# A third plain up pair, a down tile in two passes, and ScalarE copying the last mixer level

## The chip, the cores and the metric

One core of one Trainium2 chip. The metric is the device time of one execution of the whole program in microseconds (us). Engines are named as in the profile: PE is the matmul engine (TensorE), PEld its weight loads, DVE is VectorE, ACT is ScalarE, POOL is GpSimd, and SP only issues loads.

## The reference, cut to what matters

Two trunk layers run on 640 tokens: 512 latent tokens and 128 context tokens, which share the weights. Each layer normalizes x, projects it, runs four mixers in parallel (two attentions, and two gated linear recurrences, of which `chunked_gla` is the core), merges them by gates, adds to x, normalizes again and runs a ConvFFN. All is float32. The parts that the change touches:

```
scores = einsum('bnthk,bnshk,bntshk->bnhts', q, k, decay)   # within a block, masked to t >= s

h2 = rms_norm(x, norm2_g) * (1 + sc2) + sh2
u  = h2 @ w_up                       # 1024 -> 2 x 2816
u  = sum(up[:, j:j + t] * conv_w[j] for j in range(3)) + conv_b
a, g = split(u, 2)
x  = x + g2 * (silu(g) * a) @ w_down # 2816 -> 1024
```

## The kernel before, in words

Activations lie transposed: 128 channels on the partitions, 640 tokens along the row. A float32 product is made of three matmuls on rounded operands: with a value split into a rounded part ("hi") and its remainder ("lo"), hi x hi, lo x hi and hi x lo are added up in PSUM. ACT makes every hi part with a copy that rounds, DVE makes every lo part by subtracting hi from the value, and PE waits for both. Each matmul takes 128x128 weights and 320 tokens.

**Up stage.** The 2816 up channels are 22 pairs of tiles, j = 0 to 21, an `a` tile and a `g` tile each. The first N_PLAIN = 2 pairs are plain products (`two_products`, `up`, lines 789 to 791): 96 matmuls a pair. The other 20 (`strassen`, L1238 to L1240) trade matmuls for sums: a pair is seven parts of 12 matmuls, 84 in all. For this they need, once for a layer, four sums of blocks of the activation, called T here (T1 to T4), and for every pair three sums of weight blocks.

- POOL makes `weight_sums(s)` (L722 to L727, four instructions) when the weight chunk of pair s has landed, for s = 0 ahead of everything else of this stage. It then waits for the whole normalized h, adds hi and lo up again (L740) and makes the T operands (L743 to L748), then `weight_sums(1)`, and so on.
- ACT rounds weights (`up_unit` L1669, `round_sums` L1758 to L1764), rounds T (`round_t` L1768), applies the centre tap of the convolution (`centre` L1777) and the SiLU (L1782).
- DVE makes the lo parts (`up_lo` and `sums_lo`, both through L1991; `t_rest` L2403), the outer taps (`taps` L2374 and L2378), the product `gated` (L2386), and in the Strassen pairs the sums between parts (L2421 to L2459).
- Before that, DVE and ACT make h in eight tiles of 128 channels, one after the other (L1963 to L1979 on DVE, L1354 and L1363 on ACT); PE's pair 0 follows them tile by tile.

Weight chunks go through four slots of RING, loaded by SP as slots come free. A chunk's slot is free when the first matmul of the next chunk has run. Chunk j of the up stage takes the slot of the fourth chunk before it, so up chunk 2 follows the third of the four chunks of the output projection, and up chunk 3 the fourth.

**Down stage.** Eight output tiles, written as two iterations of four. Each takes 22 channel tiles f = 0 to 21 of silu(g) x a. ACT rounds each f (`round_d` L1787), DVE makes its remainder (`rest_d` L2416). For each f in turn, PE runs six matmuls: hi x hi, hi x lo and lo x hi for both token halves. The weights of a tile come in two units of 11 f (`down_unit` L1673 on ACT, `down_lo` on DVE). The first tile waits at each f for `rest_d` of that f; in the later tiles everything is there.

**Mixer, gated recurrences.** For each of three units (x = 0, 1, 2; the third has four heads, the others two) the scores are made in eight passes: pass 0, and one for each of seven levels, whose blocks double in size. PE makes the scores of a head in PSUM (L1116) and goes on with pieces of the merge products (`fill`). DVE's `keep` puts the blocks of the level into SCORE, with a copy under a mask (L2191), and counts `sc_kept`; PE's next scores, and behind the last level the transposes L1128, wait for that count. Between these calls DVE and ACT serve the merge: ACT a gate (L1620) and the rounding of the next weights (L1583), DVE the gating and the lo part.

The order on each engine is written out by hand; there is no scheduler. Everything here happens once in each of the two layers.

Of the kernel before, what the change touches and what calls it, by code (L numbers as in the profile page):

```python
# [12 lines left out]
P = 128  # L13
# [86 lines left out]
N_PLAIN, N_STRASSEN = 2, FT - 2  # L100
# [187 lines left out]
def build(nc, A, O):  # L288
    ctx = ExitStack()
    with ctx:  # L290
# [105 lines left out]
        W_SUMS = [WHI_R[:, 2560:4096], WHI_R[:, 1024:2560]]  # L396
# [30 lines left out]
        D_HI = [V_R[:, T * k:T * (k + 1)] for k in range(7)] + [HH_R[:, k, :] for k in range(KT)] + [HL_R[:, k, :] for k in range(7)]  # L427
# [117 lines left out]
        def tiles_of(w, n=P):  # L545
            return w.rearrange("p (k n) -> p k n", n=n)
# [213 lines left out]
        def _(pe):  # L760
# [3 lines left out]
            for l in range(DEPTH):  # L764
# [462 lines left out]
                def up(j):  # L1227
                    for h in range(2):
                        g = G_UP + 2 * j + h
                        wait_room(pe, l, g)  # L1230
                        lo_ready(U_UP + 2 * j + h)
                        w_hi, w_lo = up_weights(j, h, W2[h])
                        product(use(g)[0], w_hi, w_lo, h_hi, h_lo, KT, h == 0)
# [50 lines left out]
                up(1)  # L1284
                for s in range(N_STRASSEN):
                    strassen(s)
                with pe.Fori(0, 2) as it:
                    for j in range(4):
                        g = G_DOWN + j
                        wait_room(pe, l, g, it)  # L1290
                        for h in range(2):
                            lo_ready(U_DOWN + 2 * j + h, it * 8)

                            def d_lo_ready(k):
                                pe.wait_ge(d_ready, l * FT + (11 * h + k + 1))

                            product(use(g)[0], tiles_of(W_DN[h]), raw(RING_R, DOWN + 2 * j + h, 0, P, P, 11), lambda k: D_HI[11 * h + k],
                                    lambda k: ZT_R[:, 11 * h + k, :], 11, True, d_lo_ready if j == 0 else None, h == 0, h == 1)

        @block.scalar  # L1300
        def _(act):
# [17 lines left out]
            for l in range(DEPTH):  # L1319
# [305 lines left out]
                for x, g in enumerate(GLA):  # L1625
                    before = sum(y[6] for y in GLA[:x])
                    gates_before(AT[x, "turn"])
# [167 lines left out]
                silu(0)  # L1795
                round_sums(0, 0)
# [3 lines left out]
                wait_event(act, l, EV_UP + 2)  # L1800
                round_sums(0, 2)
                centre(1, 0)
                round_t("t4", 4)
                wait_event(act, l, EV_UP + 3)
                round_t("t1", 1)
                centre(1, 1)
                for s in range(N_STRASSEN):
                    if s:
                        centre(s + 1, 0)
                    wait_part(act, l, s, 0)  # L1810
                    act.activation(FIRST_A[s % 2], PS[:, use(G_UP + 2 * (N_PLAIN + s))[0], EDGE - H2:EDGE], ACT.Copy).then_inc(first_kept, 1)
                    silu(s + 1)
                    if s + 1 < N_STRASSEN:
                        round_sums(s + 1, 0)
                        round_sums(s + 1, 1)
                        wait_part(act, l, s, 5)
                        round_sums(s + 1, 2)
                    else:
                        down_unit(0)
                        wait_part(act, l, s, 5)  # L1820
                        for a, b in ((0, 4), (4, 8)):
                            act.dma_start(XT[:, a:b, :], XD.rearrange("p (k t) -> p k t", k=KT)[:, a:b, :]).then_inc(x_again, 16)
                        round_d(0, 2)
                    centre(s + 2, 1)
                round_d(2, 4)
# [3 lines left out]
                round_d(4, 6)  # L1829
                silu(FT - 1)  # L1830
                round_d(6, FT)
# [29 lines left out]
        def _(v):  # L1861
# [12 lines left out]
            for l in range(DEPTH):  # L1874
# [307 lines left out]
                def keep(x, groups, h, p):  # L2182
                    nonlocal cnt
                    v.wait_ge(sc_full, l * NSC + (cnt + 1))
                    ps = pair(3 - cnt % 2)[:, 0:T].rearrange("p (n t) -> p n t", n=NT)
                    if p == 0:
                        ins = nv.tensor_copy(SCORE[:, h], ps)
                    else:
                        v.sem_inc(scores_seen, 1)
                        m = MASK[:, p, :].rearrange("p (o t) -> p o t", o=1).to_broadcast([P, NT, P])  # L2190
                        ins = nv.copy_predicated(SCORE[:, h], m, ps)  # L2191
                    ins.then_inc(sc_kept, 1)
                    cnt += 1
                    merge_before(AT[x, 2 * groups * p + h])
# [231 lines left out]
                gated(0)  # L2426
                sums_lo(0, 0)
# [3 lines left out]
                taps(1, 0)  # L2431
# [3 lines left out]
                for s in range(N_STRASSEN):  # L2435
# [3 lines left out]
                    taps(s + 1, 1)  # L2439
# [3 lines left out]
                    if s:  # L2443
                        taps(s + 1, 0)
                    else:
                        gated(1)
# [9 lines left out]
                    else:  # L2456
                        down_lo(0)
                    wait_part(v, l, s, 5)
# [3 lines left out]
                    else:  # L2462
                        rest_d(0, 2)
                last_sum(N_STRASSEN - 1)
                rest_d(2, 4)
                taps(FT - 1, 1)
                down_lo(1)
                rest_d(4, 6)
                taps(FT - 1, 0)
                rest_d(6, FT)  # L2470
# [124 lines left out]
```

## Time and profile before

| | us |
|---|---|
| median of 3 executions | 2533.16 |
| lowest and highest | 2529.04, 2534.22 |
| the profiled execution, its own time | 2532.05 |
| its span, first to last instruction | 2529.9 |

The mean granted TensorE clock over the span is 0.974 of full speed (2.4 GHz). All positions in time below are microseconds from the start of the profiled span, and are those of the second layer, where its up stage begins near 2060 and its down stage near 2357; the first layer shows the same pattern.

### The profile page before, as it was taken

The page shows a single profiled execution, that of the slowest core. Times are in us where ns is not written, and L with a number is a line of the kernel's source. Part 1 is how long each engine was busy: PE and PEld are TensorE (multiplying, and loading weights), DVE is VectorE, ACT ScalarE, POOL GpSimd, SP SyncE. Part 2 cuts the span into 40 slices and gives each one's busy share as a digit, 9 for nine tenths or more (in the row PEclk, how much of TensorE's full clock was granted, in tenths as well). Part 3 has the DMA queues.
Part 4 walks back from the last instruction along what each step waited for, and adds up shares of the span by engine and source line. Part 5 has one row for each costly group of instructions (what it writes and reads, how often), then busy time and mean ns, then how long its engine had stood idle before and what let it go on. Part 6 is the DMA issues. An engine that isn't in the chain of part 4 may idle for free. (4 is left out here: it accounts for less than half of the span.)

```text
span 2529.9 us, 49558 instructions
## 1 busy us (share of the span) xinstructions
PE 2391.7 (95%) x21546; PEld 2224.6 (88%) x21546; DVE 1524.1 (60%) x2310; ACT 1009.8 (40%) x1384; POOL 333.3 (13%) x223
## 2 busy tenths in 40 slices
PE   5999998899999799999989999979999998999998
PEld 4999776888999799999989997768899988999998
DVE  4134476886745788883241536768775658888621
ACT  4244554322242555561143536542222544555410
POOL 0000000000000455530000000000000016555000
PEclk8999998999999999999999999989999999999999
DMA  8545111212245233333244431111222632332321
GB/s 277 190 151 184 37 46 32 54 44 53 64 144 183 59 84 84 88 100 99 75 141 126 133 93 42 48 30 51 54 65 81 212 100 62 92 89 74 99 80 65
DMA packets 326509, 239.32 MB, mean 95 GB/s; under 512 B 18272, under 2 KB 317344, under 8 KB 325024
## 3 DMA queue, kind: packets, MB, share of 16 engines
q1 hardware_dynamic: 317584, 211.32, 28.5%
q10 hardware_dynamic: 8720, 24.99, 2.9%
q8 instruction: 162, 2.65, 0.4%
q14 instruction: 43, 0.35, 0.0%
HBM read 220.68 MB, written 15.60 MB: 93 GB/s over the span
## 5 line engine op out<-in xcount | busy, mean ns | idle before, releaser
L789 PE MATMUL PS<-HH_split,WHI_split 128*128 128x320 f32 x1888 | 600.3, 318 | 13.2 <-DVE HL_split L1966 10.4
L791 PE MATMUL PS<-HH_split,RING_split 128*128 128x320 f32 x1856 | 578.0, 311 | 0.0
L790 PE MATMUL PS<-HL_split,WHI_split 128*128 128x320 f32 x1632 | 508.7, 312 | 0.0
L1991 DVE TENSOR_TENSOR RING_split<-RING,WHI_split 128x1024 fp32r<-128x1024 f32 (+2 forms) x162 | 224.9, 1390 | 262.6 <-ACT WHI_split L1673 185.1
L789 PEld LDWEIGHTS PS<-HH_split,WHI_split 128*128 128x128 f32 x1888 | 359.3, 190 | 26.6 <-issue 15.2
L790 PE MATMUL PS<-ZT_split,WHI_split 128*128 128x320 f32 x1208 | 375.9, 311 | 0.0
L791 PEld LDWEIGHTS PS<-HH_split,RING_split 128*128 128x128 f32 x1856 | 352.9, 190 | 0.0
L790 PEld LDWEIGHTS PS<-HL_split,WHI_split 128*128 128x128 f32 x1632 | 310.9, 191 | 0.3
L722 POOL TENSOR_TENSOR ST<-RING 128x512 f32<-128x512 f32 x20 | 31.9, 1595 | 1824.0 <-DMA RING<-in_w_up 1725.1
L790 PEld LDWEIGHTS PS<-ZT_split,WHI_split 128*128 128x128 f32 x1208 | 229.5, 190 | 0.0
L1239 PE MATMUL PS<-BIG_split,WHI_split 128*128 128x320 f32 x640 | 200.3, 313 | 0.0
L1998 DVE TENSOR_TENSOR RING_split<-RING,WHI_split 128x1024 fp32r<-128x1024 f32 x52 | 62.2, 1223 | 228.6 <-ACT WHI_split L1382 228.2
L789 PE MATMUL PS<-V_split,WHI_split 128*128 128x320 f32 x536 | 169.8, 317 | 8.9 <-DVE ZT_split L2416 8.9
L791 PE MATMUL PS<-V_split,RING_split 128*128 128x320 f32 x544 | 171.0, 314 | 0.0
L1238 PE MATMUL PS<-V_split,WHI_split 128*128 128x320 f32 x480 | 150.5, 313 | 18.6 <-DVE BIG_split L2403 13.8
L1620 ACT ACTIVATE WHI<-PS 128x640 f32<-128x640 f32 x48 | 33.8, 705 | 263.2 <-PE PS L791 263.0
L1673 ACT ACTIVATE WHI_split<-RING 128x1408 fp32r<-128x1408 f32 x32 | 44.1, 1379 | 214.4 <-PE PS L791 214.4
L1543 ACT ACTIVATE BIG<-PS,NMX 128x768 f32<-128x768 f32 (+1 forms) x120 | 94.1, 791 | 76.4 <-DVE NMX L2092 76.3
L1239 PEld LDWEIGHTS PS<-BIG_split,WHI_split 128*128 128x128 f32 x640 | 122.2, 191 | 0.0
L2191 DVE COPY_PREDICATED BIG<-MASK,PS 128x640 f32<-128x640 uint8 x112 | 98.3, 884 | 35.4 <-PE PS L1116 34.6
L2092 DVE TENSOR_REDUCE NMX<-PS 128x1 f32<-128x768 f32 (+1 forms) x120 | 93.3, 819 | 37.5 <-PE PS L1004 33.9
L789 PEld LDWEIGHTS PS<-V_split,WHI_split 128*128 128x128 f32 x536 | 101.9, 190 | 11.9 <-DVE ZT_split L2416 8.9
(305 smaller groups left out, 5481.5 us busy)
## 6 DMA issues: line engine op xcount, KB each, us to landing
RING<-in_w_in SPq DMA_DIRECT2D x96, 512.0 KB, 4.0
RING<-in_w_up SPq DMA_DIRECT2D x88, 512.0 KB, 5.0
RING<-in_w_ada SPq DMA_DIRECT2D x80, 512.0 KB, 6.3
RING<-in_w_down SPq DMA_DIRECT2D x32, 384.0 KB, 3.6
RING<-in_w_in SPq DMA_DIRECT2D x40, 256.0 KB, 3.3
RING<-in_w_down SPq DMA_DIRECT2D x32, 320.0 KB, 4.0
RING<-in_w_out SPq DMA_DIRECT2D x16, 512.0 KB, 4.6
ZT<-in_w_ada SPq DMA_DIRECT2D x8, 1024.0 KB, 9.2
```

The costliest lines, as they stand in the source:

```text
L789: release(pe.matmul(out, w_hi, hi[:, a:b], start=begin, stop=False), fresh and a == 0)
L790: pe.matmul(out, w_hi, lo[:, a:b], start=False, stop=False)
L791: ins = pe.matmul(out, w_lo, hi[:, a:b], start=False, stop=end)
L1238: release(pe.matmul(out, w_hi[k], hi[:, k, :], start=not onto and k == 0, stop=False, skip_group_check=onto), fresh and k == 0)
L1239: pe.matmul(out, w_hi[k], lo[:, k, :], start=False, stop=False, skip_group_check=onto)
L1543: act.activation(PROB[g % 3][m][:, 0:n], pair(m)[:, 0:n], ACT.Exp, bias=NMX[:, g % 3, m:m + 1], accum_out=SUMS[:, g % 3, m:m + 1]).then_in ...
L1620: act.activation(GATE[m % 2], acc(use(g)[0]), ACT.Sigmoid).then_inc(gemm_free[use(g)[0]], 1)
L1673: act.activation(W_DN[q % 2], RING[:, (DOWN + q) % N_SLOT, 0:11 * P], ACT.Copy).then_inc(hi_made, 1)
L1991: nv.tensor_tensor(rest, value, as_f32(hi), ALU.subtract).then_inc(lo_made, 1)
L1998: nv.tensor_tensor(z_raw(RING_R, l, c, j), z_raw(RING, l, c, j), as_f32(w_z(u, 256 if kind in ("t4", "t1") else P)), ALU.subtract).then_in ...
L2092: nv.tensor_reduce(NMX[:, g % 3, m:m + 1], pair(m)[:, 0:keys(g // NS) * P], AX.X, ALU.max, negate=True).then_inc(nmax_ready, 1)
L2191: ins = nv.copy_predicated(SCORE[:, h], m, ps)
```

## The change

Three edits, made together.

1. **N_PLAIN is 3.** Pair j = 2 becomes a plain pair, so a layer has 19 Strassen pairs. ACT, DVE and PE get its units behind those of pair 1 (`up_unit(2, .)`, `up_lo(2, .)`, `taps(1, .)` and `gated(1)`), all ahead of the rounding of the sums and of T. `weight_sums(0)` now reads up chunk 3, not 2. The `g` weights of pair 2 go to another buffer, and the two buffers of summed weights change places, so that nothing collides.
2. **The first down tile of each iteration runs in two passes** (`down_first`): for f = 0 to 21 four matmuls with the rounded f (hi x hi and lo x hi), then for f = 0 to 21 two matmuls with the remainder. In the last Strassen pair ACT now rounds f = 0 to 10 as the operands of the finished parts come free, and 11 to 13 right behind; D_HI's places are reordered for that. DVE does both halves of the last pair's taps ahead of `down_lo(1)` and of the remainders from f = 4 on.
3. **ACT copies the blocks of the last mixer level** (the seventh, two blocks of 64x64 on each of five token blocks) straight from PSUM into SCORE, without a mask; DVE only goes on with the merge there.

```diff
-N_PLAIN, N_STRASSEN = 2, FT - 2
+N_PLAIN, N_STRASSEN = 3, FT - 3
...
-        D_HI = [V_R[:, T * k:T * (k + 1)] for k in range(7)] + [HH_R[:, k, :] for k in range(KT)] + [HL_R[:, k, :] for k in range(7)]
+        D_HI = [V_R[:, T * k:T * (k + 1)] for k in range(4)] + [HH_R[:, k, :] for k in range(KH)] + [HL_R[:, k, :] for k in range(KH)] + \
+               [V_R[:, T * k:T * (k + 1)] for k in range(4, 7)] + [HH_R[:, k, :] for k in range(KH, KT)] + [HL_R[:, k, :] for k in range(KH, 7)]
...
+                def down_first(it):
+
+                    p = use(G_DOWN)[0]
+                    wait_room(pe, l, G_DOWN, it)
+                    for f in range(FT):
+                        h, k = f // 11, f % 11
+                        w_hi, w_lo = down_weights(h)
+                        if k == 0:
+                            lo_ready(U_DOWN + h, it * 8)
+                        pe.wait_ge(d_hi, l * FT + (f + 1))
+                        for a, b, o in HALVES:
+                            out = PS[:, p, o:o + HALF]
+                            release(pe.matmul(out, w_hi[:, k, :], D_HI[f][:, a:b], start=f == 0, stop=False), k + a == 0)
+                            pe.matmul(out, w_lo[:, k, :], D_HI[f][:, a:b], start=False, stop=False)
+                    for f in range(FT):
+                        h, k = f // 11, f % 11
+                        pe.wait_ge(d_ready, l * FT + (f + 1))
+                        for a, b, o in HALVES:
+                            ins = pe.matmul(PS[:, p, o:o + HALF], down_weights(h)[0][:, k, :], ZT_R[:, f, a:b], start=False, stop=f == FT - 1)
+                        if k == 10:
+                            ins.then_inc(pe_done, 1)
...
+                    for h in range(2 * g[6]):
+                        seen = 2 * NPASS * before + 2 * g[6] * LEVELS + h
+                        gates_before(AT[x, 2 * g[6] * LEVELS + h])
+                        act.wait_ge(sc_full, l * NSC + seen + 1)
+                        act.wait_ge(sc_kept, l * NSC + seen)
+                        ps = pair(3 - seen % 2)[:, 0:T].rearrange("p (n t) -> p n t", n=NT)
+                        for ks, qs in level_blocks(LEVELS):
+                            ins = act.activation(SCORE[ks, h, :, qs], ps[ks, :, qs], ACT.Copy)
...
+                    if p == LEVELS:
+                        cnt += 1
+                        merge_before(AT[x, 2 * groups * p + h])
+                        return
```

**Where instructions move.** DVE at the beginning of the up stage, from the product of pair 0 on (rows with WORK are the taps, RING_split, CACHE and ST_split are lo parts of weights, BIG_split are remainders of T). Before:

```order
L2386 TENSOR_TENSOR ZT<-WORK 128x640
L1991 TENSOR_TENSOR RING_split<-RING,CACHE_split 128x1024
L1991 TENSOR_TENSOR ST_split<-ST,WHI_split 128x1536
L2403 TENSOR_TENSOR BIG_split<-BIG,V_split 128x4x320 x2
L2374 SCALAR_TENSOR_TENSOR WORK<-PS,COLS,WORK 128x511
```

Now, from the lo part of pair 2's `g` weights on; behind pair 0's product come also, ahead of these rows, pair 2's `a` weights and four tap instructions:

```order
L2039 TENSOR_TENSOR RING_split<-RING,WHI_split 128x1024
L2426 SCALAR_TENSOR_TENSOR WORK<-PS,COLS,WORK 128x511
L2426 SCALAR_TENSOR_TENSOR WORK<-PS,COLS,WORK 128x127
L2430 SCALAR_TENSOR_TENSOR WORK<-PS,COLS,WORK 128x511
L2430 SCALAR_TENSOR_TENSOR WORK<-PS,COLS,WORK 128x127
L2438 TENSOR_TENSOR ZT<-WORK 128x640
L2039 TENSOR_TENSOR RING_split<-RING,CACHE_split 128x1024
L2039 TENSOR_TENSOR ST_split<-ST,WHI_split 128x1536
L2455 TENSOR_TENSOR BIG_split<-BIG,V_split 128x4x320 x2
```

So two lo parts, two halves of a pair's taps (eight instructions) and one product now stand ahead of the first lo part of a Strassen pair.

ACT in the last Strassen pair (WORK rows with PS are `centre`, 128x1408 is a unit of down weights, reads of ZT are `round_d`). Before:

```order
L1673 ACTIVATE WHI_split<-RING 128x1408
L1822 DMA BIG<-x_kept 128x2560 x2
L1787 ACTIVATE V_split<-ZT 128x640 x2
L1777 ACTIVATE WORK<-PS,COLS 128x640
L1787 ACTIVATE V_split<-ZT 128x640 x2
```

Now:

```order
L1708 ACTIVATE WHI_split<-RING 128x1408
L1822 ACTIVATE V_split<-ZT 128x640 x4
L1822 ACTIVATE HH_split<-ZT 128x640 x4
L1822 ACTIVATE HL_split<-ZT 128x640 x3
L1872 DMA BIG<-x_kept 128x2560 x2
L1812 ACTIVATE WORK<-PS,COLS 128x640
```

Eleven roundings now stand between the first unit of down weights and the loads of x, where before there was none.

ACT in the second unit of the recurrences, behind its last gate and weights (WHI rows). Before:

```order
L1620 ACTIVATE WHI<-PS 128x640
L1583 ACTIVATE WHI_split<-RING 128x1280
L1630 ACTIVATE BIG<-PS 128x640 x2
L1620 ACTIVATE WHI<-PS 128x640
L1583 ACTIVATE WHI_split<-RING 128x1280
```

Now:

```order
L1644 ACTIVATE WHI<-PS 128x640
L1607 ACTIVATE WHI_split<-RING 128x1280
L1658 ACTIVATE BIG<-PS 64x5x64 x4
L1665 ACTIVATE BIG<-PS 128x640 x2
L1644 ACTIVATE WHI<-PS 128x640
```

The four copies of 64 partitions serve two heads; they follow the same gate and weights as the two copies L1665 that were next before.

## Rows read from the trace of the kernel before

**Rows 1.** the page, part 1: busy us (share of the span) and instructions of each engine.

```profile
PE 2391.7 (95%) x21546; PEld 2224.6 (88%) x21546; DVE 1524.1 (60%) x2310; ACT 1009.8 (40%) x1384; POOL 333.3 (13%) x223
```

**Rows 2.** waits of PE: engine, line, waited for: us in total, times, longest.

```profile
PE PS L1238 <- DVE BIG_split L2403: 13.9, 3, 6.9
PE PS L789 <- DVE ZT_split L2416: 8.9, 6, 2.9
```

**Rows 3.** timeline of PE, second layer: start, us, line, [idle before].

```profile
2106.54 0.60 PE L1238 MATMUL PS<-V_split,WHI_split 128*128 128x320 f32 x1 [6.88 <-DVE BIG_split L2403]
...
2112.49 0.41 PE L1238 MATMUL PS<-V_split,WHI_split 128*128 128x320 f32 x1 [2.41 <-DVE RING_split L1991]
```

**Rows 4.** stretches: length, busy (instructions) of PE, PEld, DVE, ACT, POOL; granted clock; DMA.

```profile
2106.50:2109.90 3.40, 3.36 (x12) 3.17 (x12) 3.36 (x4) 0.87 (x2) 3.32 (x2) 0.50 0.00 0
2128.50:2337.90 209.40, 209.40 (x1430) 209.40 (x1429) 175.64 (x272) 105.81 (x119) 119.95 (x86) 1.00 0.30 83
2362.30:2373.10 10.80, 7.07 (x28) 6.26 (x28) 10.77 (x15) 10.80 (x18) 2.01 (x1) 0.68 0.37 120
```

**Rows 5.** timeline of SP's queue, second layer: loads of up chunks 2 and 3.

```profile
2042.75 1.10 SPq L586 DMA_DIRECT2D RING<-in_w_up  x2
...
2067.38 1.00 SPq L586 DMA_DIRECT2D RING<-in_w_up  x2
```

**Rows 6.** timeline of POOL, second layer: weight sums, then the T operands.

```profile
2048.95 1.30 POOL L722 TENSOR_TENSOR ST<-RING 128x512 f32<-128x512 f32 x1 [914.14 <-DMA RING<-in_w_up]
2050.21 1.30 POOL L723 TENSOR_TENSOR RING<-RING 128x512 f32<-128x512 f32 x1
...
2081.83 7.16 POOL L740 TENSOR_TENSOR BIG<-HH_split,HL_split 128x640 f32<-128x640 f32 x4 [27.11 <-DVE HL_split L1963]
...
2099.53 4.28 POOL L748 TENSOR_TENSOR BIG<-BIG 128x1280 f32<-128x1280 f32 x1
```

**Rows 7.** timeline of DVE beside those weight sums.

```profile
2046.90 0.82 DVE L1920 TENSOR_TENSOR WORK<-WORK 128x640 f32<-128x640 f32 x1
...
2050.65 1.54 DVE L1920 TENSOR_TENSOR WORK<-WORK 128x640 f32<-128x640 f32 x1
```

**Rows 8.** timeline of DVE, second layer, up stage.

```profile
2083.95 1.01 DVE L2374 SCALAR_TENSOR_TENSOR WORK<-PS,COLS,WORK 128x511 f32<-128x511 f32 x2 [2.20 <-ACT WORK L1777]
...
2090.32 2.40 DVE L2386 TENSOR_TENSOR ZT<-WORK 128x640 f32<-128x640 f32 x1 [0.81 <-ACT WORK L1782]
...
2103.92 4.96 DVE L2403 TENSOR_TENSOR BIG_split<-BIG,V_split 128x1280 fp32r<-128x1280 f32 x2 [2.85 <-POOL BIG L748]
...
2113.76 1.48 DVE L2403 TENSOR_TENSOR BIG_split<-BIG,HH_split 128x1280 fp32r<-128x1280 f32 x1
...
2118.01 0.82 DVE L2386 TENSOR_TENSOR ZT<-WORK 128x640 f32<-128x640 f32 x1 [0.41 <-ACT WORK L1782]
...
2119.74 1.22 DVE L1991 TENSOR_TENSOR RING_split<-RING,HL_split 128x1024 fp32r<-128x1024 f32 x1
```

**Rows 9.** timeline of DVE: the last sum of the third Strassen pair.

```profile
2148.54 0.49 DVE L2421 TENSOR_TENSOR PS<-PS,CACHE 128x320 f32<-128x320 f32 x1
```

**Rows 10.** timeline of DVE, second layer, start of the down stage.

```profile
2375.79 5.23 DVE L2416 TENSOR_TENSOR ZT_split<-ZT,HL_split 128x640 fp32r<-128x640 f32 x7
2380.94 1.62 DVE L1991 TENSOR_TENSOR RING_split<-RING,WHI_split 128x1408 fp32r<-128x1408 f32 x1
```

**Rows 11.** timeline of ACT, the same stretch.

```profile
2369.46 4.49 ACT L1787 ACTIVATE HL_split<-ZT 128x640 fp32r<-128x640 f32 x7
...
2385.30 1.38 ACT L1673 ACTIVATE WHI_split<-RING 128x1408 fp32r<-128x1408 f32 x1 [8.30 <-PE PS L791]
```

**Rows 12.** timeline of PE, second layer, second GLA unit, behind its last level.

```profile
1810.01 0.55 PE L1128 MATMUL PS<-CONST,WORK 128*128 128x128 f32 x3 [1.57 <-DVE BIG L2191]
```

**Rows 13.** timeline of ACT there, and ACT's copy of 320 columns.

```profile
1802.26 1.27 ACT L1583 ACTIVATE WHI_split<-RING 128x1280 fp32r<-128x1280 f32 x1 [1.05 <-PE PS L791]
...
2125.39 0.43 ACT L1811 ACTIVATE V<-PS 128x320 f32<-128x320 f32 x1
```

More of the change, by code:

```diff
@@ L1292, in _ @@
                             lo_ready(U_DOWN + 2 * j + h, it * 8)
[L1294 to L1298, printed above, removed]
+                            product(use(g)[0], *down_weights(2 * j + h), lambda k: D_HI[11 * h + k],
+                                    lambda k: ZT_R[:, 11 * h + k, :], 11, True, None, h == 0, h == 1)
         @block.scalar
@@ L1626, in _ @@
                     before = sum(y[6] for y in GLA[:x])
+                    for h in range(2 * g[6]):
[6 more added lines that the diff above has]
+                            ins = act.activation(SCORE[ks, h, :, qs], ps[ks, :, qs], ACT.Copy)
+                            if ks.start == 0:
+                                step.mark(ins)
+                        ins.then_inc(sc_kept, 1)
                     gates_before(AT[x, "turn"])
@@ L1795, in _ @@
                 silu(0)
+                wait_event(act, l, EV_UP + 2)
+                up_unit(2, 0)
+                centre(1, 0)
+                wait_event(act, l, EV_UP + 3)
+                up_unit(2, 1, w=W_APART)
+                centre(1, 1)
+                silu(1)
                 round_sums(0, 0)
@@ L2426, in _ @@
                 gated(0)
+                up_lo(2, 0)
+                taps(1, 0)
+                up_lo(2, 1, w=W_APART)
+                taps(1, 1)
+                gated(1)
                 sums_lo(0, 0)
@@ L2430, in _ @@
                 t_rest(1, "t3")
-                taps(1, 0)
+                taps(2, 0)
                 sums_lo(0, 2)
@@ L2438, in _ @@
                         last_sum(s - 1)
-                    taps(s + 1, 1)
+                    taps(N_PLAIN + s - 1, 1)
                     v.wait_ge(first_kept, l * N_STRASSEN + s + 1)
@@ L2457, in _ @@
                         down_lo(0)
+                        rest_d(0, 3)
                     wait_part(v, l, s, 5)
@@ L2462, in _ @@
                     else:
-                        rest_d(0, 2)
+                        rest_d(3, 4)
                 last_sum(N_STRASSEN - 1)
-                rest_d(2, 4)
                 taps(FT - 1, 1)
+                taps(FT - 1, 0)
                 down_lo(1)
-                rest_d(4, 6)
-                taps(FT - 1, 0)
-                rest_d(6, FT)
+                rest_d(4, FT)
                 v.wait_ge(x_again, l * 32 + 32)
```

44 lines of the change are left out of this document (27 added, 17 removed).

## The prediction, made before the change was run

> **What bounds the kernel now.** I read the page's busy shares first. PE is busy for 95% of the span, DVE for 60%, ACT for 40% [rows 1], so over the whole PE sets the time, and a change counts by the PE idle time that it removes, less the matmuls that it adds. The waits of PE say where it idles: 13.9 us in total before Strassen matmuls for remainders of T, 8.9 us before down matmuls for remainders of f [rows 2]. The timeline shows the first in the second layer: idle for 6.88 us, one part of 12 matmuls, idle for 2.41 us [rows 3]. The stretches add what idling does afterwards: those 12 matmuls took 3.40 us at a granted clock of 0.50, which is the 1.2 GHz level, where the steady Strassen pairs run 1430 matmuls in 209.4 us at 1.00, the 2.4 GHz level [rows 4], 0.1466 us each. So 12 matmuls are 1.76 us at the full clock and cost some 1.6 us more at the lower one. In between, PE had waited for an operand; the stretch in the down stage with such waits has a clock of 0.68 [rows 4].
>
> Both places are bounded by DVE, which makes remainders without a break, and by POOL, which makes T before it. I therefore lay out DVE's list in the new order. All places are of the second layer, and I count each gain twice.
>
> **Edit 1, the third plain pair.** A pair costs 96 x 0.1466 = 14.07 us instead of 84 x 0.1466 = 12.32: 1.76 us more matmul work for each layer. What it buys is 14 us of PE work while T is made. How much of that comes out depends on when the last remainder of T is ready.
>
> (a) A move that the diff hides. POOL's first weight sums started at 2048.95, when up chunk 2 had landed [rows 6], 6.2 us after SP issued its load at 2042.75 [rows 5]. They now need chunk 3, whose load is issued at 2067.38 [rows 5], since its slot is held by the output projection until up pair 0 begins. So they start at about 2067.4 + 6.2 = 2073.6, and lie in the middle of the normalization, where POOL was idle for 27 us [rows 6].
>
> (b) POOL and DVE hold each other up. While POOL's weight sums ran, a DVE addition of two SBUF operands took 1.54 us instead of 0.82 [rows 7]: it began at 2050.65, and ended 0.7 us after POOL's 2050.21 + 1.30 = 2051.51 [rows 6], so it was let in when POOL's instruction was over. Likewise in the up stage, a product took 2.40 us beside POOL and 0.82 without it [rows 8]. The taps, with one operand in PSUM, took 1.01 us for each two beside POOL [rows 8] and are not held up. In the normalization, DVE's instructions read two SBUF operands; half are additions or products as in rows 7, half have a scalar operand as well, a form that the trace never shows beside a busy POOL. I take them to be held up as well, as the nearest rows are. POOL's four sums of 1.30 us [rows 6] then go in one by one between DVE's, 5.2 us, of which about 1.1 falls into time in which DVE waits for ACT anyway. The last h tile is done 4.1 us later, near 2085.9 instead of 2081.8. If only the additions are held up, it is 1.3 us later.
>
> On this form the Trainium skill speaks too. "SBUF — State Buffer", section "Who interferes with whom", says that a DVE instruction with two SBUF inputs contends with a GpSimd instruction that reads SBUF, and that the second to issue blocks for the whole of the other; by that all of the normalization's instructions are held up and edit 1 gains 2.4 us, where with the additions alone held up it would gain 5.3; the trace agrees for the additions (1.54 us against 0.82), and shows nothing for the rest.
>
> (c) T. POOL takes from 2081.83 to 2099.53 + 4.28 = 2103.81 for it [rows 6], 22 us with DVE's interruptions. It now ends near 2107.9.
>
> (d) DVE's list. From the last h tile at 2081.8 to the end of the last remainder of T it needed 2113.76 + 1.48 - 2081.8 = 33.5 us [rows 8]. The new list holds in the same place two more lo parts (1.22 each), two halves of taps (four times 1.01) and a product (0.82) [rows 8], together 7.2 us. The 2.85 us for which DVE waited for T4 [rows 8] are filled by that work. Three of the new instructions have two SBUF operands and wait for POOL; followed instruction by instruction, with POOL and DVE in turn, this adds 1.2 us. So 33.5 + 7.2 - 2.85 + 1.2 = 39.1, and the last remainder is ready at 2085.9 + 39.1 = 2125.0.
>
> (e) PE then has four of the seven parts left: 48 x 0.1466 = 7.0 us, 0.35 us until the end is seen, and 1.3 us for a lower clock after its waits of about 3 and 1 us before parts 2 and 3 (less than one whole part's 1.6). The first Strassen pair, j = 3, ends at 2133.7 and the next, j = 4, at 2146.1. Before, j = 4 was the third Strassen pair and its last sum began at 2148.54 [rows 9]. **Gain: 2.4 us for each layer.** The ends: 5.3 if (b) gives 1.3 us instead of 4.1; a loss of 1.5 if PE, idle for some 6 us inside pair 0 while h is late, runs that pair at the lower clock too, so that everything behind starts about 2 us later, and POOL's turns cost DVE 2 us more.
>
> **Edit 2, the down tile.** DVE worked without a break from the last Strassen pair until its lo part for the second tile ended at 2380.94 + 1.62 = 2382.6 [rows 10]; PE ended its first tile at about 2385.0, 0.3 us before ACT saw it at 2385.30 [rows 11]. Now PE can use what is rounded. Pass 1 has 88 matmuls, 12.9 us from 2357.5, with one wait of about 0.9 us for the second half's weights; it ends near 2371.3. ACT's roundings, 0.64 us each [rows 11], keep ahead of it, eleven being done before. Pass 2 then follows `rest_d`, 5.23/7 = 0.75 us each [rows 10], and needs only 0.29 us for each f: it ends right behind DVE. DVE's list gets 4 x 0.75 = 3.0 us shorter, since four remainders now lie in the last Strassen pair, and has about 1.5 us of waiting for ACT's last two `centre`, which stand behind 14 roundings. So the second tile's lo part ends at 2382.6 - 3.0 + 1.5 = 2381.1, and the second tile starts at 2381.2 instead of 2385.0: 3.8 us. Pass 2 works PE at under half, and the clock may be down when the second tile starts: I take off 0.8 us. The first unit's weights are given free only 22 matmuls (3.2 us) before the tile's end, and ACT's 1.38 [rows 11] and DVE's 1.62 [rows 10] with handovers take 3.4; in the first iteration DVE's list hides this, in the second it is 0.1 to 0.2 us, within rounding. **Gain: 3.0 us**, ends 1.0 (a low clock for most of the second tile's first half) and 4.2.
>
> **Edit 3, the last level.** PE waited for 1.57 us before the transposes of the second unit, for DVE's masked copy of the second head, which stood behind a merge step [rows 12]. In the other two units PE did not wait there. ACT is through with its merge step at 1802.26 + 1.27 = 1803.5 [rows 13]. Four copies of 320 columns at 0.43 [rows 13] end by 1805.3, and PE's fill covers until 1808.3, so the wait goes. In the third unit the second head's copy stands behind a gate and weights, and ends some 0.4 us before PE asks for it. **Gain: 1.5 us**, ends 1.0 and 1.6. DVE's freed time in the other units is worth nothing: PE does not wait for it there.
>
> **Sum.** 2.4 + 3.0 + 1.5 = 6.9 for a layer, 13.8 us for two. The profiled execution's own time of 2532.05 (2529.9 of it the span) becomes 2518.3. The median of the runs stands 1.1 us above it; against it I forecast **2519.3 us**. About 0.2% (5 us) is what a measurement of this kernel can tell from no change.
>
> **Rivals.**
> - *Only additions are held up in the normalization.* For it: no row shows the other form beside POOL. Against it: all rows with two SBUF operands show the exclusion. Then 5.3 + 3.0 + 1.5 = 9.8, twice: 2513.6.
> - *DVE eats the third pair.* The list before the last remainder grows by 7.2 us; if POOL's turns cost 2.4 us more than I found, PE idles as long as the new pair lasts and edit 1 gives nothing: 2 x 4.5 = 9.0, 2524.2. For it: DVE is already the last to finish there.
> - *The down tile does not get shorter, as the change says it does.* Pass 2 hangs on the same 22 remainders; if the clock is low in the second tile's first half, 0.5 us are left: 2 x 4.4 = 8.8, 2524.4.
> - *Slower: the weight sums inside the normalization.* One mechanism, POOL's and DVE's turns from (b), with its place between 2073 and 2125. Edit 1 becomes a loss when the last remainder of T ends later than 2127.4, and the whole change when later than 2131.9, 6.9 us behind my figure. That needs DVE to be held up by a POOL instruction of 2.9 us at three more places. At 2134 it costs 2.1 us a layer net: 2537.4. Against it: DVE's own work is known, and each turn lets DVE in after one POOL instruction.
>
> **Chances.** Forecast 0.43, additions only 0.20, third pair eaten 0.17, down tile not shorter 0.13, slower 0.07. All but the last are faster; in the third and fourth together, or with edit 3 short of its gain, the result comes within 0.2%. So faster 0.83, same 0.10, slower 0.07. The range reaches from both good ends (2533.2 - 2 x 11.1 = 2511) to the third and fourth rival together (about 2529): 2510 to 2529.
>
> **What would show it.** In the changed profile: POOL's first sums near 2073 and DVE's normalization instructions of up to 1.9 us beside them; the last h tile near 2086; PE's 6.9 us wait before the second Strassen part gone and waits of about 3 and 1 us before the third and fourth in its place; the second down tile starting some 24 us after the last Strassen part instead of 27.7; no wait before the second unit's transposes. A last h tile later than 2090, or waits before Strassen parts of over 6 us in sum, would make edit 1 and the forecast wrong.

## The result and the profile after

The changed kernel takes 2512.65 us (median of 4 runs, 2511.16 to 2513.83) against 2532.15 us of the kernel before (4 runs, 2529.04 to 2534.22): a ratio of 0.9927, 95% interval 0.9915 to 0.9939. It is 18.5 us faster by the ratio, and the forecast of 2519.3 us promised 13.8 us. The sign and the range held, and the size did not: a quarter of the gain by the ratio, and a third of it by the stages below, was not foreseen.

Where it lies is read by stage, from the starts of the same matmul in the two traces. The stretch "up" goes from the first product with h2 to the last Strassen matmul; "down" goes from there to the 300th matmul after it; what is left is the mixers, where only edit 3 works, and there the row goes from the transposes of the first gated-recurrence unit to those of the third (200.9 and 199.6 us before, 197.5 and 196.3 after).

| us for each layer | forecast | layer 1 | layer 2 |
|---|---|---|---|
| edit 1, up: 290.3 before, 286.4 after | 2.4 | 3.8 | 3.9 |
| edit 2, down: 52.4 before, 49.35 after | 3.0 | 3.1 | 3.1 |
| edit 3, last mixer level | 1.5 | 3.35 | 3.35 |

The sum over both layers is 20.6 us; the spans differ by 2529.9 - 2509.4 = 20.5.

The busy times on the page of the changed kernel (answers to [rows 1]): PE is still at 95%, with 5 us less of busy time than before and the rest of the gain out of its idle time.

```profile
PE 2386.7 (95%) x21570; PEld 2220.7 (88%) x21570; DVE 1505.5 (60%) x2284; ACT 1019.9 (41%) x1412; POOL 318.3 (13%) x213
```

The waits of PE in the changed kernel (as [rows 2]: in total, times, longest):

```profile
PE PS L790 <- DVE HL_split L2014: 17.8, 6, 4.9
...
PE PS L1239 <- DVE RING_split L2039: 2.5, 2, 1.3
...
PE PS L1239 <- DVE BIG_split L2455: 1.6, 2, 0.8
PE PS L1310 <- DVE ZT_split L2468: 1.4, 8, 0.2
...
PE PS L1304 <- DVE RING_split L2039: 0.9, 2, 0.4
...
PE PS L1239 <- DVE ST L2506: 0.4, 2, 0.2
```

The 13.9 us before Strassen matmuls for remainders of T are 1.6, and the 8.9 us for remainders of f are 1.4. In exchange PE now waits longer for the h tiles, 17.8 us in the first line; the same line of the kernel before, in the same view:

```profile
PE PS L789 <- DVE HL_split L1966: 10.4, 6, 4.9
```

The longest of 4.9 us in that line stands in another stage, near 1296; in pair 0 of the second layer, PE's longest wait for an h tile behind the first was this one:

```profile
2075.89 0.42 PE L789 MATMUL PS<-HH_split,WHI_split 128*128 128x320 f32 x1 [1.21 <-DVE HL_split L1966]
```

**Edit 1 in the trace.** In the second layer everything starts 13.72 us earlier by now: the first product with h2 began at 2053.11 in place of 2066.83. That number is added where a time is compared with the forecast. POOL's timeline (start, us, engine, line, operation, tiles), second layer:

```profile
2059.27 1.63 POOL L723 TENSOR_TENSOR ST<-RING 128x512 f32<-128x512 f32 x1 [936.13 <-DMA RING<-in_w_up]
2060.86 1.32 POOL L724 TENSOR_TENSOR RING<-RING 128x512 f32<-128x512 f32 x1
2062.25 1.73 POOL L726 TENSOR_TENSOR ST<-ST,RING 128x512 f32<-128x512 f32 x1
2064.06 1.60 POOL L728 TENSOR_TENSOR ST<-ST,RING 128x512 f32<-128x512 f32 x1
...
2089.11 2.97 POOL L749 TENSOR_TENSOR BIG<-BIG 128x1280 f32<-128x1280 f32 x1
```

DVE beside it, and later the last remainder of T and the last sum of pair j = 4:

```profile
2059.00 2.05 DVE L2027 SCALAR_TENSOR_TENSOR WORK<-BIG,A,WORK 128x512 f32<-128x512 f32 x2
2060.97 1.89 DVE L2024 TENSOR_TENSOR WORK<-BIG,WORK 128x640 f32<-128x640 f32 x1
2062.78 3.02 DVE L2014 SCALAR_TENSOR_TENSOR HL_split<-WORK,MOD,HH_split 128x512 fp32r<-128x512 f32 x2
2065.72 1.00 DVE L2027 SCALAR_TENSOR_TENSOR WORK<-BIG,A,WORK 128x512 f32<-128x512 f32 x2
...
2070.55 0.82 DVE L2011 TENSOR_TENSOR HL_split<-BIG,HH_split 128x640 fp32r<-128x640 f32 x1 [1.43 <-ACT BIG L1387]
...
2108.75 1.49 DVE L2455 TENSOR_TENSOR BIG_split<-BIG,HH_split 128x1280 fp32r<-128x1280 f32 x1
...
2130.90 0.49 DVE L2473 TENSOR_TENSOR PS<-PS,CACHE 128x320 f32<-128x320 f32 x1
```

The sums start at 2059.27 (2073.0 on the clock of before). The form that no row of before showed beside POOL, with a scalar operand and two SBUF operands, took 2.05 and 3.02 us for two pieces while POOL's sums ran, and 1.00 once they were over. PE's timeline shows what that does to the products, and what is left in front of the Strassen parts:

```profile
2065.85 0.63 PE L790 MATMUL PS<-HH_split,WHI_split 128*128 128x320 f32 x1 [4.90 <-DVE HL_split L2014]
...
2107.49 0.41 PE L1239 MATMUL PS<-V_split,WHI_split 128*128 128x320 f32 x1 [1.20 <-DVE RING_split L2039]
...
2110.29 0.41 PE L1239 MATMUL PS<-HH_split,WHI_split 128*128 128x320 f32 x1 [0.79 <-DVE BIG_split L2455]
...
2114.28 0.41 PE L1239 MATMUL PS<-V_split,WHI_split 128*128 128x320 f32 x1 [0.21 <-DVE ST L2506]
...
2361.31 0.56 PE L1310 MATMUL PS<-ZT_split,WHI_split 128*128 128x320 f32 x2 [0.18 <-DVE ZT_split L2468]
2362.85 0.63 PE L790 MATMUL PS<-V_split,WHI_split 128*128 128x320 f32 x1 [0.97 <-DVE RING_split L2039]
```

The last two rows are the end of edit 2's first down tile and the start of the second one. PE follows DVE's last remainders there, and then waits for the lo part of the second tile's weights, which DVE makes right behind them:

```profile
2361.19 1.61 DVE L2039 TENSOR_TENSOR RING_split<-RING,WHI_split 128x1408 fp32r<-128x1408 f32 x1
```

The stretches (busy time and count of each engine, then the granted clock): behind the late h tile, the first Strassen pair, the start of the second down tile, and the third mixer unit's projection.

```profile
2066.20:2069.10 2.90, 2.90 (x12) 2.90 (x12) 2.90 (x6) 1.89 (x4) 0.00 (x0) 0.50 0.02 6
2102.60:2118.10 15.50, 13.30 (x88) 12.51 (x87) 14.92 (x21) 7.20 (x8) 0.00 (x0) 1.00 0.25 69
2362.80:2366.10 3.30, 3.25 (x12) 3.25 (x13) 2.55 (x3) 0.49 (x1) 0.00 (x0) 0.51 0.32 97
1817.90:1821.40 3.50, 3.50 (x41) 3.46 (x30) 3.31 (x5) 1.20 (x2) 0.00 (x0) 1.00 0.00 0
```

The last of these, in the kernel before, at the same place in the program:

```profile
1830.10:1833.70 3.60, 3.60 (x30) 3.56 (x19) 3.42 (x5) 0.52 (x2) 0.00 (x0) 0.53 0.02 5
```

So the clock was lower (0.50, the 1.2 GHz level) behind the h tile's new wait, and not in the first Strassen pair, where the forecast had put it; and the third mixer unit's projection, 20 us after the wait that edit 3 removes, runs at the 2.4 GHz level now, where it ran at the 1.2 GHz level before.

### The profile page after: what moved, and what is told of

It reads as the page before. It is cut to its first block and busy times, and to the rows that moved or that the text cites. A ratio compares the mean times of both kernels' runs of the same rounds, so it can differ in the third digit from the quotient of the medians.

```text
span 2509.4 us, 49596 instructions
## 1 busy us (share of the span) xinstructions
PE 2386.7 (95%) x21570; PEld 2220.7 (88%) x21570; DVE 1505.5 (60%) x2284; ACT 1019.9 (41%) x1412; POOL 318.3 (13%) x213
## 5 line engine op out<-in xcount | busy, mean ns | idle before, releaser
L790 PE MATMUL PS<-HH_split,WHI_split 128*128 128x320 f32 x1888 | 598.6, 317 | 20.0 <-DVE HL_split L2014 17.8
L791 PE MATMUL PS<-HL_split,WHI_split 128*128 128x320 f32 x1696 | 528.4, 312 | 0.0
L2039 DVE TENSOR_TENSOR RING_split<-RING,WHI_split 128x1024 fp32r<-128x1024 f32 (+2 forms) x164 | 235.9, 1440 | 265.0 <-ACT WHI_split L1708 183.5
L791 PEld LDWEIGHTS PS<-HL_split,WHI_split 128*128 128x128 f32 x1696 | 322.8, 190 | 0.3
L791 PE MATMUL PS<-ZT_split,WHI_split 128*128 128x320 f32 x1032 | 320.5, 311 | 0.0
L791 PEld LDWEIGHTS PS<-ZT_split,WHI_split 128*128 128x128 f32 x1032 | 195.3, 189 | 0.0
L1240 PE MATMUL PS<-BIG_split,WHI_split 128*128 128x320 f32 x608 | 187.8, 309 | 0.0
L790 PE MATMUL PS<-V_split,WHI_split 128*128 128x320 f32 x480 | 151.9, 316 | 2.0 <-DVE RING_split L2039 2.0
L792 PE MATMUL PS<-V_split,RING_split 128*128 128x320 f32 x488 | 153.4, 314 | 0.0
L1239 PE MATMUL PS<-V_split,WHI_split 128*128 128x320 f32 x456 | 141.3, 310 | 2.9 <-DVE RING_split L2039 2.5
L2243 DVE COPY_PREDICATED BIG<-MASK,PS 128x640 f32<-128x640 uint8 x96 | 84.8, 883 | 34.7 <-PE PS L1117 34.5
L1239 PE MATMUL PS<-HH_split,WHI_split 128*128 128x320 f32 x304 | 94.1, 310 | 1.6 <-DVE BIG_split L2455 1.6
```

Of the source, the lines that this page charges most:

```text
L790: release(pe.matmul(out, w_hi, hi[:, a:b], start=begin, stop=False), fresh and a == 0)
L791: pe.matmul(out, w_hi, lo[:, a:b], start=False, stop=False)
L792: ins = pe.matmul(out, w_lo, hi[:, a:b], start=False, stop=end)
L1239: release(pe.matmul(out, w_hi[k], hi[:, k, :], start=not onto and k == 0, stop=False, skip_group_check=onto), fresh and k == 0)
L1240: pe.matmul(out, w_hi[k], lo[:, k, :], start=False, stop=False, skip_group_check=onto)
L2039: nv.tensor_tensor(rest, value, as_f32(hi), ALU.subtract).then_inc(lo_made, 1)
```

## The experiments

Two executions of the same code differ: up to the first product with h2 the kernel before and `pair_only` are the same program, and their profiled executions stood 2.2 us apart there (831.27 and 833.51). The stretches "up" and "down" on the other hand repeat within 0.1 us from layer to layer in most kernels, so small effects are read from them. All numbers in the table are for one layer, layer 1 and layer 2; the ratio is to executions of the kernel before that were taken beside each kernel (their medians are 2529.4 to 2532.2 us), and "low clock" counts the matmuls of the second down tile's first 68 that stood 0.2 to 0.3 us apart.

| kernel | median us | ratio (95%) | up | down | low clock |
|---|---|---|---|---|---|
| before | 2532.15 | | 290.3, 290.3 | 52.4, 52.4 | 0, 0 |
| after | 2512.65 | 0.9927 (0.9915 to 0.9939) | 286.5, 286.4 | 49.3, 49.4 | 10, 11 |
| after_again | 2510.08 | 0.9922 (0.9907 to 0.9937) | 286.4, 286.5 | 49.4, 49.3 | 10, 10 |
| pair_only | 2523.86 | 0.9971 (0.9961 to 0.9980) | 286.5, 286.5 | 52.6, 52.8 | 0, 0 |
| no_down | 2517.69 | 0.9951 (0.9937 to 0.9966) | 286.4, 286.4 | 52.7, 52.8 | 0, 0 |
| one_pass | 2515.76 | 0.9938 (0.9924 to 0.9951) | 286.4, 286.4 | 51.4, 51.4 | 0, 0 |
| no_copy | 2518.95 | 0.9948 (0.9934 to 0.9963) | 286.5, 286.4 | 49.4, 49.5 | 11, 11 |
| copy_only | 2524.93 | 0.9970 (0.9958 to 0.9982) | 290.3, 290.3 | 52.4, 52.4 | 0, 0 |
| copy_x1 | 2522.74 | 0.9969 (0.9957 to 0.9981) | 290.4, 290.2 | 52.5, 52.4 | 0, 0 |
| sums_late | 2512.30 | 0.9928 (0.9914 to 0.9941) | 288.1, 288.1 | 48.0, 47.9 | 1, 1 |
| sums_late_t | 2510.56 | 0.9919 (0.9905 to 0.9932) | 285.6, 285.6 | 49.5, 49.5 | 14, 14 |
| sums1_late | 2509.85 | 0.9917 (0.9903 to 0.9931) | 285.8, 285.8 | 49.5, 49.5 | 14, 14 |
| sums_both_late | 2501.27 | 0.9880 (0.9865 to 0.9895) | 284.3, 284.3 | 48.0, 47.9 | 1, 1 |
| gate_late | 2506.78 | 0.9900 (0.9883 to 0.9918) | 283.5, 283.6 | 49.2, 50.6 | 9, 21 |

**pair_only: edit 1 alone, on the kernel before**, with the lists of ACT, DVE and PE as the change has them.

```diff
-N_PLAIN, N_STRASSEN = 2, FT - 2
+N_PLAIN, N_STRASSEN = 3, FT - 3
...
```

> The kernel before with the first edit alone (three plain pairs). Theory from the two profiles: the last sum of pair j = 4 came 3.9 us earlier for each layer in the changed kernel, so this edit is worth 7.8 us and the time should be near 2524.4 against 2532.2 of before. The prediction's own figure of 2.4 us for each layer would give 2527.4; no gain at all (third pair eaten) 2532. The last h tile should again come about 3.3 us later than before, by POOL's weight sums in the normalization.

The ratio gives 7.3 us (5.1 to 9.9), and "up" is as long as in the changed kernel, 286.5. So the 3.8 to 3.9 us for each layer belong to this edit alone.

**no_down: edit 2 undone**, with one pass and the rounding late.

> The changed kernel with the second edit undone: one pass over the first down tile, rounding late. Theory: the edit is worth what the profiles show from the end of the last Strassen part on, 3.1 us for each layer, so 2512.7 + 6.2 = 2518.9. Rival: the early end of the down tile only moves a wait further back, and the time stays within 2 us of 2512.7.

"Down" is 52.7 and 52.8 against 49.35: 3.4 us for each layer; in time 5 to 8 us, between this kernel and the two measurements of the changed one. The rival falls: what the first tile gains isn't waited for later.

**one_pass: which half of edit 2 carries it.** The rounding stays early, but the tile is made in one pass again.

```diff
-                    down_first(it)
-                    for j in range(1, 4):
+                    for j in range(4):
...
+                            product(use(g)[0], tiles_of(W_DN[h]), raw(RING_R, DOWN + 2 * j + h, 0, P, P, 11), lambda k: D_HI[11 * h + k],
...
```

> The changed kernel with the early rounding kept, but the first down tile in one pass of six matmuls for each f as before. Theory A: VectorE's list sets the end of the tile, so the four early remainders and the early rounding carry the gain; TensorE waits some 4 us for remainder 4, runs some matmuls at the lower clock, and then follows VectorE at 0.88 us for each f against 0.75, so that the second tile starts some 2 us later than with two passes but at the full clock: 1 to 4 us slower than the changed kernel in all. Theory B: the two passes carry it, and without them the edit's 3.1 us for each layer are lost: 6 us slower than the changed kernel.

"Down" is 51.4: 2.0 us more than with two passes, and 1.0 us less than before. PE's timeline of one_pass has one wait, for the first remainder behind those made early:

```profile
2348.02 0.64 PE L790 MATMUL PS<-HH_split,WHI_split 128*128 128x320 f32 x1 [5.46 <-DVE ZT_split L2446]
```

Theory A's range (1 to 4 us) holds at its upper end, and its weights are wrong: what is made early (roundings and four remainders) carries one third of the edit, the two passes two thirds, since they fill that wait with products of the rounded f.

**no_copy, copy_only and copy_x1: edit 3 undone, alone, and alone in the second of the three units.** The edit of copy_x1 in ACT's list (DVE's copy has the same condition; in copy_only it is without it):

```diff
+                    for h in range(2 * g[6] if x == 1 else 0):
...
+                        for ks, qs in level_blocks(LEVELS):
+                            ins = act.activation(SCORE[ks, h, :, qs], ps[ks, :, qs], ACT.Copy)
...
```

> The changed kernel with the third edit undone: VectorE copies the last mixer level again. Theory A: the edit is worth the wait of 1.6 us before the second unit's transposes and, behind it, 13 matmuls of the third unit's output projection at the lower clock (1.5 us), together 3.35 us for each layer: 2512.7 + 6.7 = 2519.4. Theory B, as the prediction had it: the wait alone, 1.5 us for each layer, and the clock has another cause: 2515.7.

> The kernel before with the third edit alone, in all three units. From the two profiles: 3.35 us for each layer, 6.7 us faster than before. By the prediction's term, 1.5 us for each layer, 3.0 us faster. The 1.57 us wait before the second unit's transposes should be gone in both cases; by the first figure the third unit's first output-projection matmuls run 0.147 us apart, by the second 13 of them stay at 0.267 us.

> The kernel before with ScalarE copying the last level in the second unit alone. Theory A: the lower clock in the third unit follows from the wait in the second, so the whole 3.35 us for each layer is there, 6.7 us faster than before, and the third unit's 13 matmuls run at full clock. Theory B: it is the third unit's own copy by VectorE that costs there; then 13 matmuls stay at 0.267 us and the gain is 1.8 us for each layer, 3.6 us.

The ratios give 7.6 us for copy_only (4.6 to 10.6) and 7.8 for copy_x1 (4.8 to 10.9); no_copy lies 5 to 9 us above the changed kernel. Theory A holds in each. Its mark is the granted clock in the third unit's projection, in the second layer of copy_x1:

```profile
1821.90:1825.40 3.50, 3.50 (x39) 3.46 (x26) 3.34 (x5) 1.16 (x2) 0.00 (x0) 1.00 0.01 2
```

And of no_copy:

```profile
1819.90:1823.40 3.50, 3.50 (x22) 3.50 (x15) 3.40 (x5) 0.48 (x2) 0.00 (x0) 0.54 0.01 2
```

In the three kernels with the wait (before, pair_only, no_copy) 12 to 14 matmuls there stood some 0.267 us apart, in both layers; in the eleven without it one or two at most stood 0.25 us apart. Each matmul at 0.267 in place of 0.147 us costs 0.12 us more, so 12 cost 1.45 us. The same 360 matmuls around the place, from 60 before the second unit's transposes on, took 34.8 us in both layers of the three kernels, and 31.5 us in both layers of the eleven. So wait and lower clock come and go together, by an edit in the second unit alone; whether the wait lowers the clock by itself, or by shifting PE's work behind it, no run separates. The copies in the first and third unit give nothing that the times show.

**sums_late: POOL's first weight sums behind T**, on the changed kernel.

```diff
-                weight_sums(0)
                 pool.wait_ge(h_ready, l * 16 + 16)
...
                 pool.tensor_tensor(T_RAW["t4"], T_RAW["t4"], b22, ALU.subtract).then_inc(t_made, 1)
+                weight_sums(0)
```

> The changed kernel with POOL's first weight sums moved behind the four tiles of T. Theory: beside the normalization the sums hold VectorE up, the last h tile comes 3.3 us late and TensorE then runs 12 matmuls at the lower clock, 4.6 us in all for each layer; moved away, h and T come 3.3 us earlier, the sums are made some 2 us before they are needed, and the gain is 3.3 to 4.6 us for each layer: 2503.5 to 2506. Rival: the remainders of the sums become the late ones before the second Strassen part, and what h gains is waited for there: 2512.7, or later.

The theory falls. The last h tile did come 3.3 us earlier (2068.40 - 2053.48 = 14.9 us behind the first h2 product, 2071.37 - 2053.11 = 18.3 in the changed kernel), and the wait on h tiles was 10.4 us in total again. But DVE and ACT stood before the first sums with T finished behind them in their lists, and PE waited there. On DVE's timeline of sums_late:

```profile
2096.02 2.31 DVE L2039 TENSOR_TENSOR RING_split<-RING,CACHE_split 128x1024 fp32r<-128x1024 f32 x1 [5.20 <-POOL ST L728]
```

And on PE's:

```profile
2103.72 0.60 PE L1239 MATMUL PS<-V_split,WHI_split 128*128 128x320 f32 x1 [3.25 <-DVE BIG_split L2455]
```

"Up" is 1.7 us longer; the time stays only because the second down tile ran at the full clock from its start, which shortened "down" by 1.4 us.

**sums_late_t: T2 and T3 before the first sums, in ACT's and DVE's lists.**

```diff
-                round_sums(0, 0)
-                round_sums(0, 1)
                 round_t("t2", 3)
                 round_t("t3", 2)
+                round_sums(0, 0)
+                round_sums(0, 1)
...
```

> As sums_late, with ScalarE and VectorE also taking T2 and T3 before the first weight sums instead of after them. In sums_late VectorE stood for 5.2 us before the first sums' remainder although T was done when that wait began. Theory: filled with T2's and T3's remainders, that wait gives the last remainder of T some 3.5 us earlier than in the changed kernel and a gain of about 3 us for each layer, 6 us against the changed kernel (near 2506.5). Rival: beside POOL's sums each remainder takes as long as POOL's instruction and its own together, the sums get later, and the time stays within 2 us of 2512.5.

"Up" falls by 2.5 us against sums_late, and by 0.8 against the changed kernel: the rival. POOL and DVE took turns. POOL's timeline of sums_late_t:

```profile
2097.89 2.27 POOL L724 TENSOR_TENSOR RING<-RING 128x512 f32<-128x512 f32 x1
2100.24 2.68 POOL L726 TENSOR_TENSOR ZT<-ZT,RING 128x512 f32<-128x512 f32 x1
```

And DVE's beside it:

```profile
2096.74 2.28 DVE L2039 TENSOR_TENSOR RING_split<-RING,CACHE_split 128x1024 fp32r<-128x1024 f32 x1 [2.56 <-POOL ST L728]
2098.94 2.83 DVE L2039 TENSOR_TENSOR ST_split<-ST,WHI_split 128x1536 fp32r<-128x1536 f32 x1
```

POOL's sum of 1.30 us became 2.27 and 2.68, DVE's remainders of 1.22 and 1.75 us became 2.28 and 2.83. These are the *second* weight sums, which nobody needs yet.

**sums1_late and sums_both_late: the second weight sums held back** until three remainders of T are done, in the changed kernel and in sums_late_t. after_again is the changed kernel beside them.

```diff
                     if s + 1 < N_STRASSEN:
+                        if s == 0:
+                            pool.wait_ge(t_lo, l * 4 + 3)
                         weight_sums(s + 1)
```

> The changed kernel once more, on the same chip as the two below, so that they are compared with it directly: a ratio to before of 0.9927 within 0.0012.

> The changed kernel with POOL's second weight sums held back until the third remainder of T is done. In the changed kernel they ran from 2092.0 to 2098.8, and two VectorE instructions beside them took 1.70 instead of 0.82 us and 2.31 instead of 1.22. Theory: VectorE gains those 2.0 us before the last remainder of T, TensorE's waits of 2.2 us before the Strassen parts go, and the time falls by 1.5 to 2 us for each layer, 3 to 4 us. Rival: the second sums, now made some 8 us later, hold up the second Strassen pair, and the time stays or rises.

> As sums_late_t, with the second weight sums held back in the same way. In sums_late_t the h tile was early by 4.5 us for each layer, and 3.4 of that were lost again in front of the Strassen parts, where VectorE's instructions beside the second weight sums took 2.28 instead of 1.22, 2.83 instead of 1.75 and 1.72 instead of 1.22 us. Theory: without these 2.7 us the gain on the changed kernel is 1.1 + 2.5 = 3.6 us for each layer, 7 us. Rival: TensorE waits for the first sums' remainder, which stands behind T's whatever the second sums do, and no more than 1 us for each layer is added to the 2 us in all that sums_late_t gained.

In the first, "up" is 0.65 us shorter instead of 1.5 to 2: the rival, in part. The hold-up has moved to the product of the third pair, which now runs beside the late sums, and PE waits for the sum behind it for 1.1 us instead of 0.2. PE's waits of sums_both_late show the same (in total, times, longest; 0.4, 2, 0.2 in the changed kernel):

```profile
PE PS L1241 <- DVE ST L2508: 2.2, 2, 1.1
```

With both moves "up" is 2.1 us shorter than in the changed kernel, against 3.6 expected: beside that wait, PE waits for 2.2 us in each layer for lo parts of the first Strassen pair's weights (1.2 in the changed kernel), which is the rival in part. The remainders beside which no POOL sum runs are back at their own length (DVE's timeline of sums_both_late):

```profile
2095.76 1.23 DVE L2041 TENSOR_TENSOR RING_split<-RING,CACHE_split 128x1024 fp32r<-128x1024 f32 x1 [2.56 <-POOL ST L728]
2097.27 1.76 DVE L2041 TENSOR_TENSOR ST_split<-ST,WHI_split 128x1536 fp32r<-128x1536 f32 x1 [0.29 <-ACT WHI_split L1799]
...
2107.75 1.70 DVE L2440 TENSOR_TENSOR ZT<-WORK 128x640 f32<-128x640 f32 x1 [0.41 <-ACT WORK L1819]
```

Another 1.4 us for each layer came from the clock of the second down tile, which no theory had. The time of 2501.27 us beats both kernels: 30 us under the one before, 8.8 under after_again. Of these 8.8, the two stretches show 7.0 in both layers together; the rest was not located.

**gate_late: that product behind two of the first Strassen pair's sums**, on sums_both_late.

```diff
                     if s:
                         taps(N_PLAIN + s - 1, 0)
-                    else:
-                        gated(N_PLAIN - 1)
...
                     nv.tensor_tensor(g1, U3, a1, ALU.subtract).then_inc(out_sum, 1)
+                    if s == 0:
+                        gated(N_PLAIN - 1)
```

> As sums_both_late, with VectorE's product of the third plain pair moved from before the sums of the first Strassen pair to behind two of them. In sums_both_late this product ran beside POOL's second weight sums, took 1.70 instead of 0.82 us, and TensorE waited 1.1 us in each layer for the sum behind it. Theory: the 2.2 us of that wait go and the time falls by some 2 us, a ratio to before near 0.987. Rival: the product only holds up the next pair's weight remainders instead, and the ratio stays at 0.988.

"Up" is 0.75 us shorter, and the wait is gone; but the second down tile had 9 and 21 matmuls at the lower clock, and its five runs went from 2500.27 to 2512.55. Whether it is faster stays open.

## Why the prediction was right, and what it mis-sized

- **What bounds the kernel: right.** DVE's and POOL's lists before the first Strassen pair and the first down tile set PE's idle time, and removing it there moved the whole kernel by as much.
- **Edit 1, (a): right.** Sums at 2073.0, forecast 2073.6.
- **(b): right in kind, 0.8 us off.** The form with a scalar operand is held up too, 2.05 and 3.02 us against 1.00, so the rival "only additions" is refuted, although its 2513.6 us is the nearest figure to the result. That is luck: of the 3.4 us for each layer that the forecast missed, 1.85 lie in edit 3 and at most 0.8 in (b). The last h tile ended at 2071.37 + 13.72 = 2085.1; forecast 2085.9. The rule of the Trainium skill, "SBUF — State Buffer", section "Who interferes with whom", by which all of the normalization's instructions are held up, agrees with these rows.
- **(c) and (d): 2.1 and 1.0 us too late.** T ended at 2105.8 (forecast 2107.9) and the last remainder at 2110.24 + 13.72 = 2124.0 (forecast 2125.0).
- **(e): the term that was mis-sized.** It took off 1.3 us for a lower clock after waits of 3 and 1 us. The waits were 1.20 and 0.79 us, and the clock of the stretch was 1.00. The 1.3 and the 1.0 of (d), less some 0.8 us that was not in the sum (PE's wait of 0.21 us is a part of it, the rest was not traced), are the difference between 2.4 and 3.9: the last sum of j = 4 began at 2130.90 + 13.72 = 2144.6, forecast 2146.1, before 2148.54 [rows 9].
- **Edit 2: right in kind, its size in part by luck.** The second tile began 23.3 us behind the last Strassen matmul instead of 27.9, 0.8 us better than forecast, and 11 of its matmuls at the lower clock took 1.3 us back where 0.8 had been taken off; the two misses nearly cancel in 3.1 against 3.0. As forecast, DVE's lo part for the second tile ends (2361.19 + 1.61 = 2362.80) right before that tile begins (2362.85). How the gain divides between early remainders and two passes, the prediction did not say; one_pass does.
- **Edit 3: the step that failed.** "So the wait goes" held; its price did not. "Gain: 1.5 us, ends 1.0 and 1.6" counted the wait of 1.57 us [rows 12] and nothing behind it. With the wait, PE also ran at the lower clock 20 us later: 12 to 14 matmuls at 0.267 us, some 1.45 us more; copy_x1 shows that both go by the edit in the second unit alone. From start to start the wait cost 1.73 us (1808.13 to 1810.01, where now it is 1797.74 to 1797.89), and the term measured 3.35 us. The prediction had looked for clock losses directly behind waits, in the up and down stages alone.
- **The working.** Two slips in it change nothing: the third of POOL's four sums took 1.76 us before, not 1.30, and the new work in (d) adds up to 7.3 us, not 7.2.
- **The rivals.** The third pair was not eaten (edit 1 gave more than forecast, not nothing), the down tile did get shorter, and the weight sums did not make it slower. Their cost is there all the same: the late h tile costs PE a wait of 4.9 us in place of 1.2, and 12 matmuls at the lower clock. sums_late shows why that didn't decide: the time was slack that PE otherwise spends in front of the Strassen parts.

## What to carry to other kernels

When work is taken off a late list, ask what its neighbours on the shared resource do at that time: DVE's instructions on two SBUF operands and POOL's go one at a time here (1.22 us became 2.28 beside POOL), and the best version moved both of POOL's first two weight sums out of DVE's way, the second of them a lookahead that nobody needed yet. That gave 2.1 us for each layer; another 1.4 came with the clock of the second down tile, whose cause is not known. A move that makes one operand early gains nothing until each list on the way stops waiting in its old order. And when a PE wait is priced, read the granted clock of the next PE-heavy stretch too, not only right behind the wait: a wait of 1.6 us was worth 3.35.

## What was not expected of the hardware

The lower clock 20 us behind a short wait is one: in all fourteen kernels, with the wait 12 to 14 slow matmuls, without it one or two at most, while the 1.70 us pause of PE just before them is the same in all. The other is the second down tile. Its start lies 23.3 us behind the last Strassen matmul in every kernel with two passes, with the same waits, yet between none and 21 of its matmuls ran at the lower clock (up to 2.5 us), and the number was nearly the same in both layers of all of them but gate_late. In sums_late the stretch of 3.3 us behind the tile's start holds 22 matmuls at a granted clock of 1.00, where the changed kernel has 12 at 0.51:

```profile
2364.90:2368.20 3.30, 3.27 (x22) 3.27 (x23) 2.55 (x3) 0.47 (x1) 0.00 (x0) 1.00 0.44 128
```

So the one matmul that the table counts for sums_late and sums_both_late, the first behind a wait, was at the full clock. PE's rows at that place do not differ between these kernels; what sets the number was not found.
